# The gate products of a recurrence as four 64x64 products, one in each quarter of the PE array

## The reference

```
# LRU_W = 512 channels in LRU_BLOCKS = 8 blocks of LRU_BW = 64
xb = (rmsnorm(x) @ w_in + b_in)[..., V_END:X_END]
xc = causal_conv(xb, w=conv_w, b=conv_b)            # width 4
r  = sigmoid(block_diag(xc, w_a) + b_a)             # w_a: 8 blocks of 64 x 64
ig = sigmoid(block_diag(xc, w_i) + b_i)             # w_i: 8 blocks of 64 x 64
a  = exp(-8 * r * softplus(-lam))
h_t = a_t * h_{t-1} + sqrt(1 - a_t**2) * (ig * xc)  # scan over tokens
mix = concat(attention, h * gelu(yb))               # then @ w_out, + x, rmsnorm, SwiGLU FFN (2816)
```

## Time and profile before

| what | value |
|---|---|
| median of 3 runs | 2318.13 us (2315.09 to 2318.86) |
| the profiled execution, its own time | 2319.95 us |
| its span, first to last instruction | 2318.2 us |
| granted TensorE clock, mean | 0.987 |
| PE busy | 2248.5 us, 97% of the span |
| DVE busy | 1302.2 us, 56% |
| ACT busy | 876.6 us, 38% |
| gate products L677, busy | 30.2 us in 64 records of 594 ns |

### The profile page before, as it was taken

The page is one execution under the profiler, slowest core; times in us unless marked ns, Lnnn a source line. Parts: engine busy times, 40 slices in busy tenths (PEclk is TensorE's granted clock), DMA queues, the critical chain, the costliest instruction groups (busy, mean ns, idle before and its releaser), DMA issues.

```text
span 2318.2 us, 29726 instructions
## 1 busy us (share of the span) xinstructions
PE 2248.5 (97%) x12165; PEld 1913.5 (83%) x12165; DVE 1302.2 (56%) x2146; ACT 876.6 (38%) x1348; POOL 32.5 (1%) x66
## 2 busy tenths in 40 slices
PE   6999999999999999999999999999999899999997
PEld 6777888888777888888877888888888799999997
DVE  4686535446687544445678653535668665444453
ACT  4574323224475322223466422323546532222221
POOL 1000000000000000000000000000010000000000
PEclk9999999999999999999999999999999799999998
DMA  4123222222213222222312222232231022222221
GB/s 149 55 69 114 91 98 92 93 98 91 102 49 117 98 93 92 92 99 92 108 64 91 101 92 99 89 102 89 93 123 38 29 92 86 88 89 79 98 77 63
DMA packets 58568, 207.13 MB, mean 89 GB/s; under 512 B 7341, under 2 KB 7549, under 8 KB 58416
## 3 DMA queue, kind: packets, MB, share of 16 engines
q1 hardware_dynamic: 51840, 184.57, 23.6%
q0 software_dynamic: 3936, 12.03, 1.5%
q10 hardware_dynamic: 2656, 8.62, 0.9%
HBM read 196.44 MB, written 9.77 MB: 89 GB/s over the span
## 4 chain that ended last, share of the span: by engine, by line
PE 84%; DVE 10%; ACT 4%; issue 1%; DMA 1%; ACTq 0%; POOL 0%; DVEq 0%
PE bank L535 27%; PE bank L533 27%; PE bank L534 27%; DVE s_p L1258 2%; ACT s_p L961 1%; DVE w_lo L1157 1%; DVE xc L1297 1%; PE bank L661 1%; DVE om L1326 1%; DVE pT L1277 1%; PE bank L628 1%; PE bank L583 1%; ACT L986 0%; PE bank L557 0%; DVE ii L1325 0%
## 5 line engine op out<-in xcount | busy, mean ns | idle before, releaser
L533 PE MATMUL bank<-x_hi,w_hi 128*128 128x512 f32 (+1 forms) x2320 | 824.6, 355 | 3.8 <-DVE x_lo L1187 2.7
L883 ACT ACTIVATE w_hi<-w_raw 128x1024 fp32r<-128x1024 f32 (+1 forms) x360 | 374.6, 1041 | 1180.1 <-PE bank L535 1180.0
L535 PE MATMUL bank<-x_hi,w_lo 128*128 128x512 f32 (+1 forms) x2320 | 819.2, 353 | 0.0
L534 PE MATMUL bank<-x_lo,w_hi 128*128 128x512 f32 (+1 forms) x2320 | 818.1, 353 | 0.0
L1157 DVE TENSOR_TENSOR w_lo<-w_raw,w_hi 128x1024 fp32r<-128x1024 f32 (+1 forms) x360 | 431.9, 1200 | 136.7 <-ACT w_hi L883 135.9
L533 PEld LDWEIGHTS bank<-x_hi,w_hi 128*128 128x128 f32 x2320 | 438.2, 189 | 79.2 <-issue 13.0
L534 PEld LDWEIGHTS bank<-x_lo,w_hi 128*128 128x128 f32 x2320 | 438.4, 189 | 61.8 <-issue 1.4
L535 PEld LDWEIGHTS bank<-x_hi,w_lo 128*128 128x128 f32 x2320 | 437.7, 189 | 60.9
L533 PE MATMUL bank<-a_hi,w_hi 128*128 128x512 f32 (+1 forms) x1200 | 426.9, 356 | 6.1 <-DVE a_lo L1561 1.8
L535 PE MATMUL bank<-a_hi,w_lo 128*128 128x512 f32 (+1 forms) x1200 | 424.4, 354 | 0.0
L534 PE MATMUL bank<-a_lo,w_hi 128*128 128x512 f32 (+1 forms) x1200 | 423.7, 353 | 0.0
(11 more groups left out here) (240 smaller groups left out, 1470.9 us busy)
## 6 DMA issues: line engine op xcount, KB each, us to landing
w_raw<-in_units SPq DMA_DIRECT2D x296, 512.0 KB, 3.2
w_raw<-in_units SPq DMA_DIRECT2D x64, 448.0 KB, 3.1
x_tok<-in_x_prompt POOLq DMA_DIRECT2D x16, 512.0 KB, 5.9
out_y_p<-y_tok ACTq DMA_DIRECT2D x16, 512.0 KB, 2.6
gfin<-in_g_fin POOLq DMA_DIRECT2D x1, 512.0 KB, 6.9
kc_tok<-in_cache_k POOLq DMA_DIRECT2D x1, 512.0 KB, 6.2
vc_tok<-in_cache_v POOLq DMA_DIRECT2D x1, 512.0 KB, 7.2
out_nk_s<-in_cache_k POOLq DMA_DIRECT2D x1, 496.0 KB, 6.5
```

Source lines behind the costliest of these rows:

```text
L533: nc.tensor.matmul(out, h, hi[:, kt, c0:c1], start=(first and kt == kts[0]), stop=False)
L534: nc.tensor.matmul(out, h, lo[:, kt, c0:c1], start=False, stop=False)
L535: mm = nc.tensor.matmul(out, l, hi[:, kt, c0:c1], start=False, stop=(kt == kt_of[u] - 1))
L883: w_hi_ready.by(A(w_hi[:, u % RING, 0:n], w_raw[:, u % RAW, 0:n], ACT.Copy))
```

## The change

For each gate n (0 for `ra`, 1 for `ii`) the one 128x128 matmul becomes two of 64x64, one for each block on the diagonal. The rows (partitions of the input) of `half` 0 are 0 to 63, those of `half` 1 are 64 to 127. Gate 0 writes each half to the same half of `S[0]`; gate 1 writes it to the other half of `S[1]`. The four products of a set so use four different quarters of the array. ACT reads the second gate back crosswise, in two instructions of 64 partitions in place of one of 128. The products of the sampled tokens (L797) stay as they are.

```
                     sc_read.wait(pe, b, 2 * c + 2)
                     for n in range(2):
-                        mm = nc.tensor.matmul(S[n][:, :], gates_w[:, n, c, :], xc[:, c % 2, :],
-                                              start=True, stop=True)
+                        for half in range(2):
+                            r = slice(half * HEAD, (half + 1) * HEAD)
+                            to = (half + n) % 2 * HEAD
+                            mm = nc.tensor.matmul(S[n][to:to + HEAD, :], gates_w[r, n, c, r], xc[r, c % 2, :],
+                                                  start=True, stop=True)
                     gates_done.by(mm)
...
                     chain.link(A(ra[:, :], S[0][:, :], ACT.Tanh, bias=lru_c[:, 0, c:c + 1], scale=0.5))
-                    gates_read.by(A(ii[:, :], S[1][:, :], ACT.Tanh, bias=lru_c[:, 1, c:c + 1], scale=0.5))
+                    for half in range(2):
+                        r = slice(half * HEAD, (half + 1) * HEAD)
+                        ins = A(ii[r, :], S[1][(1 - half) * HEAD:(2 - half) * HEAD, :], ACT.Tanh,
+                                bias=lru_c[r, 1, c:c + 1], scale=0.5)
+                    gates_read.by(ins)
```

## The result

The changed kernel takes 2325.3 us (median of 8 runs) against 2317.91 for the kernel before, run beside it: a ratio of 1.0032, with a 95% interval of 1.0022 to 1.0042, so 7.4 us slower. (One run of each kernel was disturbed, 2751.7 and 2440.39, and the ratio leaves them out.) I had predicted 2317.5, with a range of 2313.5 to 2323. The prediction was wrong: the time lies outside its range, and the kernel moved the other way. The profiled execution took 2324.13 us, with a span of 2322.3 and a mean granted clock of 0.984 (0.987 before).

A forecast was written before the change was run, and what follows sets the result against it. PE was taken to bound the FFN and projections, DVE and ACT most of the mixers. Gains of 0.2 and 0.45 us, with ACT's added half at zero, gave 2318.13 - 0.65 = 2317.5 us, range 2313.5 to 2323.

The forecast's parts named there:

- All four quarters run together: Gate products on PE: the four 64x64 quarters overlap, so a set takes 1.27 us, saving 0.45.
- Rivals 1 to 3: Gate products: only row halves together (+0.41 a set, chance 0.14), bank order (+1.27, 0.04), one after the other (+2.13, 0.04).
- rival 2: Gate products: row halves writing one bank must follow one another, +1.27 us a set, 2324 us; chance 0.04.
- Rival 4: PE bounds the kernel after all, so the sets save 7.2 us wherever they stand: 2310.9; chance 0.05.
- A half of `ii` costs nearly what the whole did: ACT's gate reads: a half takes nearly 0.69 us, so the second adds 0.59 a set, 9.4 over 16 sets.
- L628 will wait for about 0.6 us, six or seven times ... cost zero, hidden by DVE's own work: PE's scores of even steps wait for `ii`; cost zero, or 7 x 0.6 = 4.2 us if uncovered.
- The cover of 0.70: PE's L644 of the following step waits for L963, leaving 0.70 us spare, in which the 0.6 wait fits.
- ACT's own list ... even at the tightest set of chunks 0 to 2. Zero: ACT's L979 to L968 come 0.59 us later, absorbed by 0.91 idle before the exponentials L961: cost zero.
- Rival 6, the clock: Mixers: longer PE waits before L661 make the clock fall, +3 to +10 us, around 2323; chance 0.06.
- Chunk 0 of block 0: Gate set on the chain: PE reaches scores and projection 0.45 us earlier; the block gains 0.2.
- Chunk 3 of block 3: Gate set on the chain: the whole 0.45 us saved on PE passes, kept but for 0.02 despite ACT's 0.59.

The follow-up runs named there:

- e2: The changed kernel with `S[1]` read whole by ACT in one instruction, so the halves of `ii` come out exchanged: 2320.21 us, 1.0003 to the kernel before.
- e3: The kernel before with four 64x64 products a set, both gates straight on the array's diagonal, ACT reading each gate in one instruction: 2317.02 us, ratio 0.9997.
- e4: The changed kernel with each set of four gate products issued twice, ACT's crosswise halves kept: 2321.17 us, 1.0016 to the kernel before.
- e5: The kernel before with ACT reading `ii` in two straight halves in chunk 3 only (step 7 of each block): 2321.76 us, ratio 1.0015.
- e7: The changed kernel with ACT doing `pT`, the next weights and `a_hi` ahead of the gates in step 7: 2321.84 us, 1.0015 to the kernel before.
- e6: The kernel before with ACT reading `ii` in two straight halves in chunks 1 and 2 only: 2321.47 us, ratio 1.0018.

## Why the prediction was wrong

**"All four quarters run together": right.** 1.27 us was forecast for the set, 1.02 measured; the overhead of the small tile is 0.16 beside the two steps of 0.43, not 0.41. Rivals 1 to 3 fall with it. For rival 2, the trace shows two row halves writing different halves of the partitions of one bank, 7 ns apart. The Trainium skill, "TensorEngine Tiling (Array Packing)", section "Gotcha 1: PSUM Pressure", says that different row tiles cannot use one bank at the same time; for this layout the measurement decides against it. Rival 4, PE as the bound, falls by e2 and e3, whose sets differ by 0.85 us and whose ratios both include 1.

**"A half of `ii` costs nearly what the whole did": right, its step mis-sized.** I took 0.59, the distance to a following instruction, with 0.69 as the upper bound, and 0.82 was measured, 0.99 by the time of `a_hi` in step 7. A half takes 0.68 to 0.69; the two halves don't overlap each other, and the instruction behind them doesn't overlap the second.

**"L628 will wait for about 0.6 us, six or seven times ... cost zero, hidden by DVE's own work": the waits right (8 times, 0.6), the zero wrong through the clock.** The cover of 0.70 is enough at 2.4 GHz: e4 has these waits at full clock, and DVE's starts don't move. It isn't enough when L628 then runs at 1.2 GHz and takes 2.0 us: the chain turns from DVE to PE. I had priced the wait and the clock apart, each against the same cover.

**"ACT's own list ... even at the tightest set of chunks 0 to 2. Zero": this is the first step that failed.** I searched chunks 0 to 2 up to the exponentials, and chunk 3 only in block 3. Chunk 3 of blocks 0 to 2 was in neither list. There DVE idled 0.63 for ACT's `a_hi` in the kernel before: the row that says "no spare" was in the trace. It costs 0.96 in each block, 2.9 us by the DVE starts; e5 lost 3.1 by it and e7 won 3.5 back. So of the sum, -0.65 us, this term alone, put at zero, was larger than the sum and of the other sign.

**Rival 6, the clock: the right place, too small a chance.** I gave it 0.06, with +3 to +10 and "around 2323". The falls cost 2.2 us in the profiled pair. I had counted only the 0.45 that PE gains before L661; but PE now idles twice ahead of these scores, 1.0 to 1.5 us for `a_tok` and then up to 0.6 for `ii`. Ahead of the chunk 1 and 2 scores one wait was traded for two.

**The gains.** Chunk 0 of block 0: 0.2 forecast; the difference in DVE's starts grows from -0.8 at 44 us, ahead of the mixers, to -1.0 at 101. Chunk 3 of block 3: 0.45 forecast, 0.05 measured from the set to the next L670, since ACT's second half entered the chain there (0.70 won, 0.65 paid). I had the two sides there as -0.45 and +0.59, and held that DVE's own work hid the second.

**Open.** Why the clock falls where it does is not shown. e5 does the same work as the kernel before up to step 7 of block 0; in both, PE waits for `a_tok` ahead of the scores of step 6 (0.98 and 0.97 us), and in e5 the clock falls behind it, from 136.5, while in the kernel before it doesn't. So a new stretch in one profile need not be the edit's doing. That the edits move the clock at all rests on all the executions: 0.983 to 0.985 in the changed kernel, 0.986 to 0.990 with its PE time filled again. e7 has more half clock in blocks 0 to 2 than the changed kernel and is faster. The 3.2 us that remain in e7 are not divided between stages: its profiled execution loses 3.9 in blocks 0 to 2 and gets 2.2 back in block 3. And of the 7.4 us between the medians the profiled pair places 5.1 in blocks 0 to 2 (2.9 for step 7, 2.2 for the clock); the rest stays open.

## What to carry to other kernels

When work moves from the busiest engine to one with spare time, follow that second engine's list through every copy of the stage, the last chunk of each block too, and look for rows where someone already waits for it: any idle time of a third engine with its name in the brackets means that the spare is zero there. A saving on an engine that then waits is worth nothing, and where the engine's clock can fall it can cost: price an added wait and a fall of the clock together, against one cover. An edit that helps in only two of its sixteen places can be confined to them; here even that was worth nothing measurable (0.9996).

When two profiles are compared, follow the start of the same instruction through both, at a place without idle time behind it: a late start that the next wait swallows costs nothing. Executions of one kernel also differ in where the clock falls, so compare the granted clock of all of them before a stretch in one profile is put down to the edit.

## What the hardware showed

- Eight float32 passes of 64x64 products with 512 columns, in all four quarters, take 1.02 us; in two quarters at a time (e3) 1.87; as four full passes of 128x128, 1.72.
- An ACT instruction on 64 partitions with 512 columns takes 683 ns against 0.69 us on 128, and two in a row take 1.38. The instruction behind starts 1.41 us after the first of the two, where it started 0.59 after a single one. Groups of the changed kernel (count, then busy and mean ns):

```profile
L980 ACT ACTIVATE ii<-bank,lru_c 64x512 f32<-64x512 f32 x32 | 21.9, 683 | 0.7
```

- More work on PE made the kernel faster (e4 against the changed kernel, 1.0016 against 1.0032), with 10 us less at 1.2 GHz in blocks 0 to 2 of the profiled execution.
- A stretch at 1.2 GHz costs nothing where other engines hold the chain (two of 3.4 us in e2 and two in e5, under 0.05 us each) and 1.3 us where PE comes onto it (6.8 us in e2). Where PE is on the chain already, 3.4 us cost 1.6 (e6, step 7 of block 1).
